# Two product lengths of an input unit, alternated or in two blocks

## The chip, the cores and the metric

The kernel runs on one core of a Trainium2 chip. A core has a matrix engine (TensorE, PE in the profile, with its weight loads as PEld), a vector engine (VectorE, DVE), a scalar engine (ScalarE, ACT), a general engine (GpSimd, POOL) and a queue for transfers (SyncE, SP). They run side by side and wait for one another by semaphores. The metric is device time in microseconds; the median of three runs of the kernel before is 1085.15 us (1085.05 to 1085.44).

## The reference

Three layers act on a sequence of 256 tokens with 1024 features, all in float32. The first has sliding-window attention and a feed-forward part, the second a gated mixing of chunks (gating stage below) and a feed-forward part, the third a mixer of a state-space scan and attention, and an MLP. The parts that the change touches:

```python
def conv_gated_ffn(h, w_in, conv_w, conv_b, w_out):
    S = h.shape[1]
    g, u = jnp.split(h @ w_in, 2, axis=-1)
    gp = jnp.pad(g, ((0, 0), (CONV_WIDTH - 1, 0), (0, 0)))
    g = conv_b + sum(conv_w[k] * gp[:, k:k + S] for k in range(CONV_WIDTH))
    return (jax.nn.gelu(g) * u) @ w_out

def chunked_sgu(h, w_in, ln_g, ln_b, w_s, b_s, w_out):
    z = jax.nn.gelu(h @ w_in)
    u, v = jnp.split(z, 2, axis=-1)
    ...
    return (u * sv.reshape(B, S, SGU_HALF)) @ w_out
...
    f = jnp.square(jax.nn.relu(h @ w_up[i])) @ w_down[i]
```

The inner size of a feed-forward part is 2816 (22 tiles of 128, each with a gate and an up half), that of the gating stage's u half 3072 (24 tiles), that of the MLP 4096 (32 tiles).

## The kernel before

All weights stream through a ring of six buffers in units of 128 partitions by 1024 values. SyncE loads a unit into `raw`; ScalarE rounds it to the short format of the matrix engine (`w_hi`, line 151); VectorE subtracts to get the rest (`w_lo`, line 156). The activations are kept in the same two parts, `a_hi` and `a_lo`, side by side in one tensor `both`. A product of two float32 numbers is then the sum of three: hi x hi, hi x lo and lo x hi.

`features_apart` computes one unit of an input projection: 128 output features for 256 tokens, a sum over KT = 8 slices of 128 input features. Its stationary operand is a slice of the weights. Since `w_hi` meets both parts of the activations, one product of 512 columns takes both at once (the two halves of a PSUM bank); `w_lo` meets `a_hi` alone, in a product of 256 columns that adds to the first half. The two halves are added later by ScalarE and VectorE. So a unit is sixteen products, eight long (line 198) and eight short (line 200), here called pairs. `pre` is given by no caller.

Who calls it: the feed-forward loop of `ffn_pe` (two units for tile t, gate and up, then `accumulate` for the down projection of tile t - 2, twelve products of 512 columns at line 251); the gating stage, 24 units, twenty of them in a row (`u_unit`); `mlp_pe` (one unit for tile t, then twelve products for an earlier tile). That makes 42 + 42 + 24 + 30 = 138 units. The last tiles of a feed-forward part and of the MLP are held: their input units stand together, and the down projections follow in one block.

The order on each engine is written out by hand. A unit waits for `lo_done` (its `w_lo` is ready) before its first product, and its last product raises `unit_used`, which lets ScalarE overwrite the ring buffer and read the results. The other products of the kernel are `three` (lines 173 to 175), which uses 256 columns for features and 512 or 256 for tokens.

Of the kernel before, what the change touches and what calls it, by code (L numbers as in the profile page):

```python
# [13 lines left out]
P = 128  # L14
SEQ = 256
TT = SEQ // P
D = 1024
KT = D // P
# [68 lines left out]
def build(nc, w, x_in, cols_in, misc_in, tables_in, rows_in, ws_in, wdt_in, out):  # L87
    def sb(name, shape, dt=F32):
        return nc.alloc_sbuf_tensor(name, shape, dt)
# [9 lines left out]
    w_hi = sb("w_hi", [P, RING, UNIT], F32R)  # L99
    w_lo = sb("w_lo", [P, RING, UNIT], F32R)  # L100
# [3 lines left out]
    both = sb("both", [P, 2, 2 * KT, SEQ], F32R)  # L104
    a_hi, a_lo = both[:, 0], both[:, 1]
# [10 lines left out]
    ps = nc.alloc_psum_tensor("ps", [P, 8, 512], F32)  # L116
# [73 lines left out]
    def features_apart(pe, n, bank, i=0, pre=None):  # L190

        s = n % RING
        pe.wait_ge(lo_done, n + 1 + RING * i)
        for k in range(KT):
            if pre is not None:
                pe.wait_ge(pre.lo, pre.base + k + 1)
            c = slice(k * P, (k + 1) * P)
            pe.matmul(ps[:, bank, :].rearrange("p (h t) -> p h t", h=2), w_hi[:, s, c], both[:, :, k, :],  # L198
                      start=k == 0, stop=False)
            mm = pe.matmul(ps[:, bank, 0:SEQ], w_lo[:, s, c], a_hi[:, k, :], start=False, stop=k == KT - 1)  # L200
        mm.then_inc(unit_used, 1)

    def features_tile(pe, n, bank, tt, pre, ks=range(KT)):
# [176 lines left out]
    def tile(tt):  # L380
        return slice(tt * P, (tt + 1) * P)
# [196 lines left out]
    def ffn_in_pe(pe, f, n0, t, i=0):  # L578
        if t >= 3:
            pe.wait_ge(f.summed, t - 1 + 2 * i)  # L580
        g_bank, u_bank = f_banks(t, i)
        features_apart(pe, f_g(n0, t), g_bank, i)
        features_apart(pe, f_g(n0, t) + 1, u_bank, i)
# [5 lines left out]
    def ffn_pe(pe, f, n0, u, following, turn_early=True):  # L589
        entry_pe(pe, u, n0, f_banks(0, 0))  # L590
        features_apart(pe, f_g(n0, 1), f_banks(1, 0)[0])
        row_pe(pe, u, 2)
        features_apart(pe, f_g(n0, 1) + 1, f_banks(1, 0)[1])
        ffn_in_pe(pe, f, n0, 2)
        pe.wait_ge(next_sems.row_out, f_row[f])
        pe.wait_ge(f.lo, 1)
        accumulate(pe, f_out(n0, 0), f_slot(0), True, False)
        ffn_in_pe(pe, f, n0, 3)
        pe.wait_ge(f.lo, 2)
        accumulate(pe, f_out(n0, 1), f_slot(1), False, False)  # L600
        with pe.Fori(0, (FT - 6) // 2) as i:
            for t in (4, 5):
                ffn_in_pe(pe, f, n0, t, i)
                pe.wait_ge(f.lo, t - 1 + 2 * i)
                accumulate(pe, f_out(n0, t - 2), f_slot(t), False, False, i)
        ffn_in_pe(pe, f, n0, FT - 2)
        ffn_in_pe(pe, f, n0, FT - 1)
        held = [(f_out(n0, t), f_slot(t)) for t in range(FT - HELD, FT)]
        held_pe(pe, following, held, lambda slot: pe.wait_ge(f.lo, FT - HELD + [s for _, s in held].index(slot) + 1), turn_early)
# [1882 lines left out]
```

## Time and profile before

| | |
|---|---|
| median of 3 runs | 1085.15 us |
| the profiled execution | 1085.08 us, span 1083.1 us |
| TensorE busy | 1064.0 us, 98% |
| weight loads | 902.2 us, 83% |
| VectorE | 820.6 us, 76% |
| ScalarE | 673.4 us, 62% |
| GpSimd | 39.8 us, 4% |
| DMA, mean over the span | 171 GB/s |

Busy time is the union of an engine's instructions. A matmul's recorded time overlaps the next one's, so the number of products times a mean duration is more than the time that they take. The distance between two starts, which a timeline gives, is the pace.

### The profile page before, as it was taken

The page shows a single profiled execution, that of the slowest core. Times are in us where ns is not written, and L with a number is a line of the kernel's source. Part 1 is how long each engine was busy: PE and PEld are TensorE (multiplying, and loading weights), DVE is VectorE, ACT ScalarE, POOL GpSimd, SP SyncE. Part 2 cuts the span into 40 slices and gives each one's busy share as a digit, 9 for nine tenths or more (in the row PEclk, how much of TensorE's full clock was granted, in tenths as well). Part 3 has the DMA queues.
Part 4 walks back from the last instruction along what each step waited for, and adds up shares of the span by engine and source line. Part 5 has one row for each costly group of instructions (what it writes and reads, how often), then busy time and mean ns, then how long its engine had stood idle before and what let it go on. Part 6 is the DMA issues. An engine that isn't in the chain of part 4 may idle for free. (4 is left out here: it accounts for less than half of the span.)

```text
span 1083.1 us, 18647 instructions
## 1 busy us (share of the span) xinstructions
PE 1064.0 (98%) x6022; PEld 902.2 (83%) x6022; DVE 820.6 (76%) x1460; ACT 673.4 (62%) x1270; POOL 39.8 (4%) x71
## 2 busy tenths in 40 slices
PE   7999999999999999999999999999999999999997
PEld 7978888888788888888888888899668888888886
DVE  6777998888754678877998888798779749666664
ACT  6567564555765867666554555777877747445553
POOL 0010000000010002220000000000000000000000
PEclk9999999999999999999999999999999999999999
DMA  8363666556366565443665565264212545655541
GB/s 333 130 230 127 204 201 206 175 191 196 118 233 202 168 213 169 162 169 112 204 203 204 175 193 195 81 220 167 78 40 82 184 145 173 201 188 186 185 151 40
DMA packets 51380, 185.04 MB, mean 171 GB/s; under 512 B 5728, under 2 KB 6240, under 8 KB 51328
## 3 DMA queue, kind: packets, MB, share of 16 engines
q1 hardware_dynamic: 49248, 178.28, 49.1%
q0 software_dynamic: 1504, 5.44, 1.4%
q8 instruction: 31, 0.51, 0.2%
q10 hardware_dynamic: 576, 0.64, 0.2%
q14 instruction: 21, 0.17, 0.1%
HBM read 183.29 MB, written 1.05 MB: 170 GB/s over the span
## 5 line engine op out<-in xcount | busy, mean ns | idle before, releaser
L156 DVE TENSOR_TENSOR w_lo<-raw,w_hi 128x1024 fp32r<-128x1024 f32 x336 | 411.7, 1233 | 74.2 <-ACT w_hi L151 70.8
L151 ACT ACTIVATE w_hi<-raw 128x1024 fp32r<-128x1024 f32 x336 | 350.8, 1053 | 70.6 <-PE ps L251 44.5
L198 PE MATMUL ps<-both,w_hi 128*128 128x512 f32 x1104 | 392.3, 398 | 0.9 <-DVE arena L656 0.9
L200 PE MATMUL ps<-both,w_lo 128*128 128x256 f32 x1104 | 309.7, 281 | 0.0
L251 PE MATMUL ps<-w_hi,both 128*128 128x512 f32 x992 | 292.9, 395 | 1.1 <-DVE both L2209 0.5
L198 PEld LDWEIGHTS ps<-both,w_hi 128*128 128x128 f32 x1104 | 207.3, 188 | 51.7 <-DVE arena L656 1.8
L251 PEld LDWEIGHTS ps<-w_hi,both 128*128 128x128 f32 x992 | 178.8, 188 | 39.1 <-issue 1.2
L200 PEld LDWEIGHTS ps<-both,w_lo 128*128 128x128 f32 x1104 | 208.4, 189 | 2.5
L251 PE MATMUL ps<-w_lo,both 128*128 128x512 f32 x496 | 158.2, 392 | 0.0
L251 PEld LDWEIGHTS ps<-w_lo,both 128*128 128x128 f32 x496 | 93.1, 188 | 21.2
L621 ACT ACTIVATE arena<-arena 128x256 f32<-128x256 f32 x44 | 18.4, 419 | 98.9 <-DVE arena L652 98.9
L173 PE MATMUL ps<-both,w_hi 128*128 128x256 f32 x256 | 74.2, 290 | 1.0 <-DVE arena L424 0.7
L174 PE MATMUL ps<-both,w_hi 128*128 128x256 f32 x256 | 72.4, 283 | 0.0
L175 PE MATMUL ps<-both,w_lo 128*128 128x256 f32 x256 | 72.4, 283 | 0.0
L173 PE MATMUL ps<-w_hi,both 128*128 128x512 f32 (+1 forms) x160 | 61.2, 382 | 0.6 <-DVE both L460 0.6
L175 PE MATMUL ps<-w_hi,both 128*128 128x512 f32 (+1 forms) x160 | 59.1, 369 | 0.0
L174 PE MATMUL ps<-w_lo,both 128*128 128x512 f32 (+1 forms) x160 | 59.0, 369 | 0.0
L173 PEld LDWEIGHTS ps<-both,w_hi 128*128 128x128 f32 x256 | 48.9, 191 | 3.8 <-issue 2.4
L652 DVE SCALAR_TENSOR_TENSOR arena<-pad,cols,arena 128x256 f32<-128x256 f32 x88 | 42.7, 485 | 10.2 <-DVE arena L648 0.3
L174 PEld LDWEIGHTS ps<-both,w_hi 128*128 128x128 f32 x256 | 49.0, 191 | 0.2
L175 PEld LDWEIGHTS ps<-both,w_lo 128*128 128x128 f32 x256 | 48.9, 191 | 0.0
L2190 ACT ACTIVATE arena<-ps 128x256 f32<-128x256 f32 x32 | 12.2, 382 | 49.8 <-PE ps L200 49.8
(212 smaller groups left out, 1206.8 us busy)
## 6 DMA issues: line engine op xcount, KB each, us to landing
raw<-in_w SPq DMA_DIRECT2D x336, 512.0 KB, 3.4
row<-in_rows POOLq DMA_DIRECT2D x7, 512.0 KB, 4.4
x<-in_x SPq DMA_DIRECT2D x2, 512.0 KB, 4.4
out<-x SPq DMA_DIRECT2D x4, 256.0 KB, 2.0
misc<-in_misc POOLq DMA_DIRECT2D x1, 512.0 KB, 6.1
arena<-in_ws POOLq DMA_DIRECT2D x1, 512.0 KB, 9.1
tab<-in_tables POOLq DMA_DIRECT2D x1, 320.0 KB, 4.8
tab<-in_tables POOLq DMA_DIRECT2D x1, 256.0 KB, 5.3
```

The lines of the kernel that those rows point to most:

```text
L151: act.activation(w_hi[:, s, :], raw[:, s, :], ACT.Copy).then_inc(hi_done, 1)
L156: dve.tensor_tensor(w_lo[:, s, :], raw[:, s, :], w_hi[:, s, :].bitcast(F32), ALU.subtract).then_inc(lo_done, 1)
L173: pe.matmul(o, l_hi, r_hi, start=first, stop=False)
L174: pe.matmul(o, l_hi, r_lo, start=False, stop=False)
L175: return pe.matmul(o, l_lo, r_hi, start=False, stop=last)
L198: pe.matmul(ps[:, bank, :].rearrange("p (h t) -> p h t", h=2), w_hi[:, s, c], both[:, :, k, :], start=k == 0, stop=False)
L200: mm = pe.matmul(ps[:, bank, 0:SEQ], w_lo[:, s, c], a_hi[:, k, :], start=False, stop=k == KT - 1)
L251: mm = pe.matmul(ps[:, 2 * tt + c, :], a[:, slot, t], b[:, s, c * 512:(c + 1) * 512], start=f, stop=z)
L621: act.activation(F_GL[:, b, :], F_CV[:, b, :], ACT.Gelu_apprx_tanh).then_inc(f.gelu, 1)
L652: dve.scalar_tensor_tensor(F_CV[:, b, :], pad[:, b, k:k + SEQ], col(k), F_CV[:, b, :], ALU.mult, ALU.add).then_inc(f.conv, 1)
L2190: act.activation(M_PT[:, t % 3, :], ps[:, m_bank(t, i), SEQ:2 * SEQ], ACT.Copy).then_inc(m_sem.part, 1)
```

## The change

The one loop over k becomes two: the eight products with `w_hi` first, then the eight with `w_lo`. The slice `c` is written as `tile(k)`, which is the same slice.

```diff
--- before.py
+++ after.py
@@ -194,10 +194,10 @@
         for k in range(KT):
             if pre is not None:
                 pe.wait_ge(pre.lo, pre.base + k + 1)
-            c = slice(k * P, (k + 1) * P)
-            pe.matmul(ps[:, bank, :].rearrange("p (h t) -> p h t", h=2), w_hi[:, s, c], both[:, :, k, :],
+            pe.matmul(ps[:, bank, :].rearrange("p (h t) -> p h t", h=2), w_hi[:, s, tile(k)], both[:, :, k, :],
                       start=k == 0, stop=False)
-            mm = pe.matmul(ps[:, bank, 0:SEQ], w_lo[:, s, c], a_hi[:, k, :], start=False, stop=k == KT - 1)
+        for k in range(KT):
+            mm = pe.matmul(ps[:, bank, 0:SEQ], w_lo[:, s, tile(k)], a_hi[:, k, :], start=False, stop=k == KT - 1)
         mm.then_inc(unit_used, 1)
 
     def features_tile(pe, n, bank, tt, pre, ks=range(KT)):
```

The order on TensorE in the MLP loop, before: the end of one down projection and the start of the next unit (`mlp_lo` and `mlp_summed` are raised by VectorE).

```order
L251 MATMUL ps<-w_hi,both 128x512 x2
L193 REGISTER_ALU [waits mlp_summed]
L198 MATMUL ps<-both,w_hi 128x512 [waits lo_done]
L200 MATMUL ps<-both,w_lo 128x256
L198 MATMUL ps<-both,w_hi 128x512
L200 MATMUL ps<-both,w_lo 128x256
L198 MATMUL ps<-both,w_hi 128x512
L200 MATMUL ps<-both,w_lo 128x256
```

The pairs go on until there are eight. The same place after:

```order
L251 MATMUL ps<-w_hi,both 128x512 x2
L193 REGISTER_ALU [waits mlp_summed]
L197 MATMUL ps<-both,w_hi 128x512 [waits lo_done]
L197 MATMUL ps<-both,w_hi 128x512 x7
L200 MATMUL ps<-both,w_lo 128x256 x8
L2169 REGISTER_ALU
L245 REGISTER_ALU [waits mlp_lo]
L251 MATMUL ps<-w_hi,both 128x512 [waits lo_done]
```

The long products of the unit now follow the long ones of line 251 without a short one between them, and the short ones stand in one block ahead of the next down projection. The wait for `lo_done` is where it was. 

Where units follow each other directly, TensorE at tile 2 of the first feed-forward, from the gate unit to the up unit, before:

```order
L200 MATMUL ps<-both,w_lo 128x256
L198 MATMUL ps<-both,w_hi 128x512
L200 MATMUL ps<-both,w_lo 128x256
L198 MATMUL ps<-both,w_hi 128x512 [waits lo_done]
L200 MATMUL ps<-both,w_lo 128x256
L198 MATMUL ps<-both,w_hi 128x512
```

and after:

```order
L200 MATMUL ps<-both,w_lo 128x256 x8
L197 MATMUL ps<-both,w_hi 128x512 [waits lo_done]
L197 MATMUL ps<-both,w_hi 128x512 x7
L200 MATMUL ps<-both,w_lo 128x256 x8
L251 MATMUL ps<-w_hi,both 128x512 [waits lo_done,ffn0_lo,next_row_out]
```

Here a block of short products is followed by the long block of the next unit. The gating stage has twenty units in this way. VectorE, ScalarE, GpSimd and the transfer queue have the same instructions in the same order as before.

## Rows read from the trace of the kernel before

**Rows 1.** The page: busy us (share) x instructions; the granted clock in 40 slices.
```profile
PE 1064.0 (98%) x6022; PEld 902.2 (83%) x6022; DVE 820.6 (76%) x1460; ACT 673.4 (62%) x1270; POOL 39.8 (4%) x71
...
PEclk9999999999999999999999999999999999999999
```

**Rows 2.** The page, costliest groups: busy us, mean ns; idle before, releaser.
```profile
L198 PE MATMUL ps<-both,w_hi 128*128 128x512 f32 x1104 | 392.3, 398 | 0.9 <-DVE arena L656 0.9
L200 PE MATMUL ps<-both,w_lo 128*128 128x256 f32 x1104 | 309.7, 281 | 0.0
```

**Rows 3.** Waits of TensorE: us in total, times, longest us.
```profile
PE ps L281 <- DMA tab<-in_tables: 4.7, 1, 4.7
...
PE ps L198 <- DVE arena L656: 0.9, 2, 0.5
```

**Rows 4.** Busy time by windows: a feed-forward turn, an MLP turn.
```profile
core 0: us, PE busy (x) PEld busy (x) DVE busy (x) ACT busy (x) POOL busy (x), PEclk, DMA share, GB/s
132.90:141.28 8.38, 8.38 (x45) 7.15 (x44) 7.35 (x13) 4.22 (x7) 0.00 (x0) 1.00 0.63 207
943.42:949.01 5.59, 5.59 (x30) 4.70 (x28) 3.63 (x6) 2.81 (x4) 0.00 (x0) 1.00 0.56 188
```

**Rows 5.** Timeline of TensorE (start us, us), end of the MLP.
```profile
1072.43 0.62 PE L251 MATMUL ps<-w_hi,both 128*128 128x512 f32 x2
...
1077.19 0.39 PE L251 MATMUL ps<-w_hi,both 128*128 128x512 f32 x1
```

**Rows 6.** The same in the second mixer, two lengths in blocks.
```profile
720.70 0.40 PE L173 MATMUL ps<-w_hi,both 128*128 128x512 f32 x1
...
722.54 0.39 PE L175 MATMUL ps<-w_hi,both 128*128 128x512 f32 x1
...
723.45 0.28 PE L173 MATMUL ps<-both,w_hi 128*128 128x256 f32 x1
...
724.40 0.28 PE L175 MATMUL ps<-both,w_lo 128*128 128x256 f32 x1
...
726.32 0.38 PE L1491 MATMUL ps<-tab,arena 128*128 128x128 f32 x2
```

**Rows 7.** The same in the gating stage.
```profile
360.75 0.40 PE L198 MATMUL ps<-both,w_hi 128*128 128x512 f32 x1
...
364.28 0.40 PE L198 MATMUL ps<-both,w_hi 128*128 128x512 f32 x1
```

**Rows 8.** The same in the first units of a feed-forward.
```profile
104.95 0.39 PE L198 MATMUL ps<-both,w_hi 128*128 128x512 f32 x1
...
112.58 0.63 PE L251 MATMUL ps<-w_hi,both 128*128 128x512 f32 x2
```

**Rows 9.** The same in one turn of the MLP loop.
```profile
943.42 0.39 PE L198 MATMUL ps<-both,w_hi 128*128 128x512 f32 x1
943.64 0.28 PE L200 MATMUL ps<-both,w_lo 128*128 128x256 f32 x1
...
944.11 0.40 PE L198 MATMUL ps<-both,w_hi 128*128 128x512 f32 x1
944.35 0.28 PE L200 MATMUL ps<-both,w_lo 128*128 128x256 f32 x1
944.47 0.40 PE L198 MATMUL ps<-both,w_hi 128*128 128x512 f32 x1
...
946.23 0.64 PE L251 MATMUL ps<-w_hi,both 128*128 128x512 f32 x2
...
948.09 0.63 PE L251 MATMUL ps<-w_lo,both 128*128 128x512 f32 x2
...
949.01 0.39 PE L198 MATMUL ps<-both,w_hi 128*128 128x512 f32 x1
```

**Rows 10.** The same, first products of two feed-forward turns.
```profile
132.90 0.39 PE L198 MATMUL ps<-both,w_hi 128*128 128x512 f32 x1
...
141.28 0.39 PE L198 MATMUL ps<-both,w_hi 128*128 128x512 f32 x1
```

## The prediction

> **What bounds the kernel now.** I read the page's busy shares first: TensorE is busy 1064.0 of 1083.1 us, 98%, VectorE 76%, ScalarE 62% [rows 1]. The clock digits are all nines and each stage I asked for has a granted clock of 1.00, the 2.4 GHz level [rows 1, 4]. So a gain has to come from TensorE's own pace, and it arrives at the end unless another engine takes its place. Next the waits of TensorE: the longest is 4.7 us for the first table, and at the two lines that the change touches there are 0.9 us in all [rows 3]. The windows then show the inner loops: in one turn of a feed-forward pair of units and in one of an MLP unit TensorE is busy without a hole (8.38 of 8.38 us, 5.59 of 5.59), while VectorE has 7.35 and 3.63 of work and the DMA share is 0.63 and 0.56 [rows 4]. TensorE is the bound there, with about 1 us to spare on VectorE in the tighter of the two.
>
> A busy sum can't price this change: matmuls overlap, the mean of one is 398 ns for 512 columns and 281 ns for 256 [rows 2], yet a pair takes much less than 679 ns. What counts is the distance from start to start, so I took starts from timelines.
>
> **The paces that the trace shows.** (a) A settled stream of 512-column products: 21 of them between 1072.43 and 1077.19, 4.76 us, 0.2267 each [rows 5]. (b) A stream of 256-column products: 24 from 723.45 to 726.32, 2.87 us, 0.120 each; the first eight behind a long block take 0.95 [rows 6]. (c) 512-column products directly behind 256-column ones: the first eight take 1.84 (720.70 to 722.54), the next four 0.91, so 0.03 us is lost at the start of such a block and nothing later [rows 6]. Eight settled ones take 8 x 0.2267 = 1.81. (d) The alternation of today: ten pairs from 360.75 to 364.28 take 3.53, 0.353 a pair [rows 7]; (a) and (b) add to 0.2267 + 0.120 = 0.347. So changing length at each instruction costs 0.006 us a pair. (e) Not everywhere: in the first units of a feed-forward, 22 pairs from 104.95 to 112.58 take 7.63, 0.347, the plain sum [rows 8]. This also tells me that the two-piece moving operand of the long product (the high and the low half of the activations) costs nothing of its own, since in (e) these same products run at the pace of (a) and (b). (f) The 512-column stream behind an alternating unit pays too: its first eight take 946.23 to 948.09, 1.86 [rows 9].
>
> **The change part by part.** It removes nothing and adds nothing: 1104 products of each length as before [rows 2]. The wait for the weights stays ahead of a unit's first product and the signal that the unit is used stays on its last; both loops run over the same weights. Each unit goes from eight pairs to one block of eight 512s and one of eight 256s. VectorE, ScalarE and the DMA queue keep their order; each of them only sees the end of the unit, which comes sooner. A unit now has one change to long and one to short in place of fifteen.
>
> MLP turn (one unit, then twelve long products of the down projection): now 943.42 to 949.01, 5.59 [rows 9]. After: the unit's long block follows a long stream, 1.81; its short block 0.95; the twelve behind it 1.84 + 0.91 = 2.75; sum 5.51. Saves 0.08. There are 28 such units: 2.2 us.
>
> Feed-forward turn (two units, then twelve): now 132.90 to 141.28, 8.38 [rows 10]. After: 1.81 + 0.95 for the first, 1.84 + 0.95 for the second (behind short ones), 2.75: 8.30. Saves 0.08; 17 turns in each of two layers: 34 x 0.08 = 2.7 us.
>
> Gating stage, twenty units in a row at pace (d): 8 x 0.353 = 2.82 each, after 1.84 + 0.95 = 2.79. Saves 0.03 x 20 = 0.7 us. (With a third digit, 2.824 against 2.79.)
>
> The last four units of a feed-forward, and the last two of the MLP, stand together in front of held products: 4 x 2.82 = 11.29 becomes 2.76 + 3 x 2.79 = 11.13, 0.16 twice, and 2 x 2.82 becomes 2.76 + 2.79, 0.1: 0.4 us in all.
>
> Units that already run at (e): four in each feed-forward and the last four of the gating stage, 12: 8 x 0.347 = 2.77 becomes 2.79. Costs 0.02 x 12 = 0.2 us.
>
> Sum: -2.2 - 2.7 - 0.7 - 0.4 + 0.2 = -5.8 us. The profiled execution took 1085.08 us, its span 1083.1 and 2.0 around it; the median of the runs is 1085.15, so nothing need be shifted. 1085.1 - 5.8 = 1079.3 us, 0.53% faster.
>
> Bounds of the one unknown. No row shows blocks of exactly eight and eight. If a change of length cost nothing, each unit would take 2.77 and the result would be lower by 0.03 us for each of 138 units with two changes, some 4 us less at most: 1075. If each long block of a unit paid what the eight of (f) pay, it would take 1.86 in place of 1.81 or 1.84, at most 0.05 x 138 = 6.9 us more, which eats the gain: 1086. I take (c), because it is the nearest row: the same two lengths, weights new for each product, in one accumulation after another.
>
> What hides the rest: the loops would run at 8.30 and 5.51, above VectorE's 7.35 and 3.63 [rows 4], so its work stays covered; at its own busy time it would bind only after another 0.9 us. Between stages TensorE waits for chains that start at its own last product, and those move with it.
>
> A rule to weigh: the Trainium skill, "TensorE: Matmul & The Clock Gate", section "Back-to-back issue gap", gives columns over 2.4 plus 2.5 ns at the full clock, by which a pair would take 325 ns in any order and the change would be worth nothing. Neither (a), 0.2267, nor the pair at 0.353 agrees: the trace has an excess per product, and one that depends on the order.
>
> **The rivals.** *No change.* The delay of a long product could belong to something other than the neighbour, so that each block of eight starts afresh as in (f): 1.86 + 0.95 = 2.81 against 2.82, and behind the short block the twelve still pay as today. Saves 0.01 x 138 = 1.4 at most; I put it at 1084.3. For it: the trace has two paces for the same alternation, (d) and (e), and I can't say what sets one or the other. Against it: rows 6 and 5 settle after a few products.
>
> *Slower.* One mechanism, at each unit: the weight load. A short product leaves little time to bring the next weights in. Now each short one is followed by a long one, under which a load fits easily; in a block of short ones each load stands under a short product, at 0.120 against the 0.117 at which the short ones go in the alternation (944.35 to 944.47, 0.12) [rows 9]. If the long ones keep what they have in a pair, 0.353 - 0.117 = 0.236 (944.11 to 944.35, 0.24), for a reason of their own, a unit takes 8 x 0.236 + 8 x 0.120 = 2.85 against 2.82: +0.024 x 126 units = +3.0, 1088.1 us. It decides where a long product inside a block stays above 0.233. For it: the short stream's 0.120 is measured. Against: (e), and the 0.2267 at a unit's edge, where a long product follows a long one (943.42 to 943.64).
>
> The Trainium skill speaks against the change here: "TensorE: Matmul & The Clock Gate", section "LDWEIGHTS (loading the stationary operand)", puts a load of 128 columns at 128 / 1.2 = 107 ns, as long as a 256-column product streams, so a block of short ones would have no slack at all; the same rule adds nothing beyond the 0.120 of (b), which is in the sum already.
>
> *Part of it is given back.* The feed-forward loops could fall on VectorE, whose 7.35 of 8.38 is a mean and has chains in it (convolution, gelu, product). Then 2.7 us stay away: 1082.0. Against: no wait of TensorE on VectorE shows inside a loop.
>
> **How the numbers follow.** Forecast 0.70, part given back 0.08, no change 0.13, slower 0.09. The smallest difference from no change that a measurement of this kernel can tell is about 0.2%, 2.2 us. Faster: 0.70 + 0.08, and nothing of the rest: 0.78; same 0.13; slower 0.09. The likeliest case alone spans 1077.3 to 1081.0. The range reaches up to the no-change case to leave out only the slower one and a tail: 1077.0 to 1084.6.
>
> **What would show it.** In the changed profile, a unit's eight long products behind a long stream should take 1.81 from its first start to the start of the short block, 1.84 behind short ones, the short block 0.95; the MLP turn 5.51, the feed-forward turn 8.30. Mean duration and count of the two groups say little. I am wrong if long products in the middle of a block stay at 0.235, if the turns are unchanged, or if TensorE shows waits on VectorE at the down projection's first product in the loops.

## The result

| | |
|---|---|
| changed kernel, median of 5 | 1079.27 us (1079.23 to 1079.37) |
| before, median of 5 beside it | 1085.15 us (1085.05 to 1085.46) |
| ratio | 0.9945 [0.9934, 0.9957] |
| profiled execution | span 1077.4 us (1083.1 before) |

The change makes the kernel 5.9 us, 0.55%, faster; the forecast was 5.8 us and 1079.3.

The page of the changed kernel, busy times and the groups of TensorE (as in [rows 1, 2]):

```profile
PE 1058.5 (98%) x6022; PEld 903.8 (84%) x6022; DVE 820.3 (76%) x1460; ACT 673.8 (63%) x1270; POOL 40.0 (4%) x71
...
L251 PE MATMUL ps<-w_hi,both 128*128 128x512 f32 x992 | 292.6, 395 | 1.1 <-DVE both L2209 0.5
L197 PE MATMUL ps<-both,w_hi 128*128 128x512 f32 x1104 | 275.4, 391 | 0.9 <-DVE arena L656 0.9
...
L200 PE MATMUL ps<-both,w_lo 128*128 128x256 f32 x1104 | 153.9, 282 | 0.0
```

TensorE is busy 5.5 us less and still 98% of the span. The groups show how little the busy column can tell of a pace: the short products go from 309.7 to 153.9 us and the long ones from 392.3 to 275.4, since products of one line that follow each other are now merged where they overlap. The means are 391 and 282 ns against 398 and 281 [rows 2]. The pace has to be read from starts. One turn of the MLP loop in the timeline of TensorE (start us, us; it answers to [rows 9]):

```profile
939.48 1.98 PE L197 MATMUL ps<-both,w_hi 128*128 128x512 f32 x8
941.29 1.11 PE L200 MATMUL ps<-both,w_lo 128*128 128x256 f32 x8
942.25 0.63 PE L251 MATMUL ps<-w_hi,both 128*128 128x512 f32 x2
...
944.09 0.62 PE L251 MATMUL ps<-w_lo,both 128*128 128x512 f32 x2
...
945.00 0.39 PE L197 MATMUL ps<-both,w_hi 128*128 128x512 f32 x1
```

Eight long products behind a long stream take 941.29 - 939.48 = 1.81, the eight short ones 942.25 - 941.29 = 0.96 (0.95 and a rounding), the first eight long ones behind them 1.84, and the turn 5.52 in place of 5.59. A feed-forward turn (answers to [rows 10]):

```profile
124.46 1.98 PE L197 MATMUL ps<-both,w_hi 128*128 128x512 f32 x8
126.28 1.12 PE L200 MATMUL ps<-both,w_lo 128*128 128x256 f32 x8
127.23 2.00 PE L197 MATMUL ps<-both,w_hi 128*128 128x512 f32 x8
129.07 1.12 PE L200 MATMUL ps<-both,w_lo 128*128 128x256 f32 x8
130.02 0.63 PE L251 MATMUL ps<-w_hi,both 128*128 128x512 f32 x2
...
132.77 0.39 PE L197 MATMUL ps<-both,w_hi 128*128 128x512 f32 x1
```

1.82, 0.95, 1.84, 0.95 and 2.75 add to 8.31; before it was 8.38. TensorE in this window, and VectorE beside it:

```profile
core 0: us, PE busy (x) PEld busy (x) DVE busy (x) ACT busy (x) POOL busy (x), PEclk, DMA share, GB/s
124.46:132.77 8.31, 8.31 (x46) 7.17 (x44) 7.90 (x14) 4.64 (x8) 0.00 (x0) 1.00 0.71 232
```

VectorE's 7.90 is 95% of this window, which lies near the stage's start, and TensorE still has no hole. The next turn (132.77 to 141.08) has 7.15.

Where the 5.7 us of the two spans lie, from starts in the two timelines: from the first product of a stage's first unit to the first product behind its last unit.

| stage, us | before | changed | moved | forecast |
|---|---|---|---|---|
| first feed-forward | 169.01 | 167.51 | -1.50 | -1.4 |
| gating, 24 units | 69.55 | 68.90 | -0.65 | -0.6 |
| second feed-forward | 168.86 | 167.53 | -1.33 | -1.4 |
| MLP | 163.06 | 160.78 | -2.28 | -2.3 |

### The profile page after: what moved, and what is told of

Read it like the earlier page. It is cut to its first block and busy times, and to the rows that moved or that the text cites. A ratio compares the mean times of both kernels' runs of the same rounds, so it can differ in the third digit from the quotient of the medians.

```text
span 1077.4 us, 18647 instructions
## 1 busy us (share of the span) xinstructions
PE 1058.5 (98%) x6022; PEld 903.8 (84%) x6022; DVE 820.3 (76%) x1460; ACT 673.8 (63%) x1270; POOL 40.0 (4%) x71
## 5 line engine op out<-in xcount | busy, mean ns | idle before, releaser
L197 PE MATMUL ps<-both,w_hi 128*128 128x512 f32 x1104 | 275.4, 391 | 0.9 <-DVE arena L656 0.9
L197 PEld LDWEIGHTS ps<-both,w_hi 128*128 128x128 f32 x1104 | 202.4, 188 | 40.7 <-DVE arena L656 1.7
L200 PEld LDWEIGHTS ps<-both,w_lo 128*128 128x128 f32 x1104 | 150.6, 190 | 10.8
L200 PE MATMUL ps<-both,w_lo 128*128 128x256 f32 x1104 | 153.9, 282 | 0.0
L175 PE MATMUL ps<-both,w_lo 128*128 128x256 f32 x256 | 72.4, 283 | 0.0
L173 PEld LDWEIGHTS ps<-both,w_hi 128*128 128x128 f32 x256 | 49.0, 191 | 3.6 <-issue 2.2
L174 PEld LDWEIGHTS ps<-both,w_hi 128*128 128x128 f32 x256 | 49.0, 192 | 0.2
L175 PEld LDWEIGHTS ps<-both,w_lo 128*128 128x128 f32 x256 | 49.0, 191 | 0.0
```

Source lines behind the costliest of these rows:

```text
L173: pe.matmul(o, l_hi, r_hi, start=first, stop=False)
L174: pe.matmul(o, l_hi, r_lo, start=False, stop=False)
L175: return pe.matmul(o, l_lo, r_hi, start=False, stop=last)
L200: mm = pe.matmul(ps[:, bank, 0:SEQ], w_lo[:, s, tile(k)], a_hi[:, k, :], start=False, stop=k == KT - 1)
```

## The experiments

Each stands against the kernel before, run beside it on the same chip. Below, a return is a change from short products to long ones, and the settled paces are (a) and (b) of the prediction. My theory is the forecast's: a long product behind short ones comes late, by an amount that dies away over some six of them, and each return pays this once. The rivals: something other than length costs (the change of the weight tensor, the columns of the bank), or only long blocks gain.

### One part alone: the MLP

```diff
 # mlp_pe
-            features_apart(pe, m_up(t), m_bank(t, i), i)
+            features_blocks(pe, m_up(t), m_bank(t, i), i)
 # features_blocks: the changed features_apart; all others keep the old one
```

> Only the MLP's 30 units go in two blocks; feed-forward and gating stay alternated. Theory (a change from short to long costs some 0.03 us at the start of the long block, wherever it is, and the stages are independent): the MLP turn goes from 5.59 to 5.51 us, the other turns stay at 8.38 and at 0.353 a pair, the time falls by 2.3 us to 1082.8. Rival (the gain comes from one stage's waits, or a gain in one stage is given back by the ring of weights in another): the turn is 5.51 but the total moves by less than 1.5 us.

Measured 1082.84 against 1085.0 (ratio 0.9979 [0.9970, 0.9988]): 2.2 us less, the MLP's share of the table. The first and the last row of a turn:

```profile
937.55 1.98 PE L210 MATMUL ps<-both,w_hi 128*128 128x512 f32 x8
...
943.06 0.39 PE L210 MATMUL ps<-both,w_hi 128*128 128x512 f32 x1
```

5.51. The other stages keep their lengths in its trace (169.00, 69.55 and 169.05), and what TensorE saves in the MLP arrives at the end, but for 0.1 us.

### Is it the weight tensor or the length? All products long

```diff
-            mm = pe.matmul(ps[:, bank, 0:SEQ], w_lo[:, s, tile(k)], a_hi[:, k, :], ...)
+            mm = pe.matmul(ps[:, bank, :].rearrange("p (h t) -> p h t", h=2), w_lo[:, s, tile(k)], both[:, :, k, :], ...)
```

once in the order of before and once in two blocks of eight.

> The order of before, but the product with the weights' low part takes both parts of the activations too, so that all sixteen products of a unit have 512 columns (one term more is summed than before). Theory (only a change of length costs): every product goes at 0.2267 inside a unit, a unit takes 3.63 whatever the order, and the time is that of the blocked order of the same products within 1 us; about 1085 + 138 x 0.81 = 1197 us. Rival (the price comes from changing between the two weight tensors at each product): the alternated kernel is slower than the blocked one by 5 to 7 us.

> All sixteen products of a unit have 512 columns as in the run beside it, eight with the high part of the weights first, then eight with the low part. Theory (only a change of length costs): 0.2267 a product, the same time as the alternated order within 1 us, about 1197 us. Rival (changing the weight tensor costs): faster than the alternated order by 5 to 7 us.

Measured 1191.68 (alternated) and 1191.53 (blocks), ratios to before 1.0979 [1.0962, 1.0996] and 1.0979 [1.0962, 1.0995]. The order makes no difference as soon as the lengths are equal. Alternated, gating stage, from one high product to the one eight pairs on:

```profile
420.19 0.39 PE L196 MATMUL ps<-both,w_hi 128*128 128x512 f32 x1
420.42 0.39 PE L199 MATMUL ps<-both,w_lo 128*128 128x512 f32 x1
...
423.82 0.39 PE L196 MATMUL ps<-both,w_hi 128*128 128x512 f32 x1
```

423.82 - 420.19 = 3.63 for sixteen products, 0.2267 each. In blocks, eight of them:

```profile
420.82 1.98 PE L196 MATMUL ps<-both,w_hi 128*128 128x512 f32 x8
422.63 1.75 PE L199 MATMUL ps<-both,w_lo 128*128 128x512 f32 x7
```

1.81. So changing between the two weight tensors at each product is free. The total is 5 us under my 1197: I had left out that the down projections no longer come behind short products and lose their own delay. The twelve take 949.01 - 946.23 = 2.78 in [rows 9] and 12 x 0.2267 = 2.72 here; at some 65 places that is 4 us. Most of the rest is rounding: a unit grew by 3.63 - 2.824 = 0.80 and not by 0.81, which is 1 us over 138 units.

### Is it the bank's columns?

```diff
-            mm = pe.matmul(ps[:, bank, 0:SEQ], w_lo[:, s, c], a_hi[:, k, :], ...)
+            mm = pe.matmul(ps[:, bank, SEQ:2 * SEQ], w_lo[:, s, c], a_hi[:, k, :], ...)
```

> The order of before; the short products add to the second half of the bank in place of the first (the halves are summed later, so the result is the same sum). Theory (length of the neighbours): nothing changes, 1085.1, 0.353 a pair. Rival (the price of the alternation comes from adding to columns of the bank that the long product has just written, or is still writing): the pace moves; with the second half the columns are the ones written last, so the pair gets longer, by over 0.005 us, and the time by over 5 us.

Measured 1085.26 against 1085.0, ratio 1.0001 [0.9992, 1.0010]. Ten pairs in the gating stage:

```profile
361.68 0.40 PE L196 MATMUL ps<-both,w_hi 128*128 128x512 f32 x1
...
365.21 0.40 PE L196 MATMUL ps<-both,w_hi 128*128 128x512 f32 x1
```

3.53, as in [rows 7]. Which half of the columns just written the short product adds to does not matter.

### The size of the blocks

```diff
+        for k0 in range(0, KT, G):
+            for k in range(k0, k0 + G):
                 pe.matmul(... w_hi ...)
+            for k in range(k0, k0 + G):
                 mm = pe.matmul(... w_lo ...)
```

with G = 4 and G = 2; G = 8 is the changed kernel.

> All units in the order 4 long, 4 short, 4 long, 4 short. Theory (the delay of long products dies away over about six of them, 6, 9, 2, 5, 4 ns): four long ones behind short ones take 0.930, four short ones 0.472, a unit behind short ones 2.80 against 2.79 with blocks of eight: 1.5 to 2 us slower than the blocks of eight, 1081.0. Rival 1 (a fixed price of 0.020 for each return to long): 2.81 a unit, 1082.0. Rival 2 (only blocks long enough to settle gain anything): 1085.

> All units in the order 2 long, 2 short, four times. Theory (dying delay): two long ones behind short ones 0.469, two short ones 0.232, a unit 2.80: 1081 to 1082. Rival 1 (a fixed price of 0.020 for each return to long): 4 x 0.020 = 0.08 a unit, more than the alternation's 0.05: 1087. Rival 2 (only long blocks gain): 1085.

Measured, against 1085.0: G = 4 1082.24 (0.9972 [0.9961, 0.9983]), G = 2 1078.44 (0.9938 [0.9924, 0.9952]). Both lie outside what I wrote for the theory, on opposite sides, and neither rival fits both: a fixed price of 0.020 gives 1082.0 for four, which is near, and 1087 for two, which is far off; "only long blocks gain" gives 1085 for either. The timelines tell where the theory went wrong. With G = 4, the second half of an MLP unit and the twelve behind it:

```profile
943.11 1.09 PE L196 MATMUL ps<-both,w_hi 128*128 128x512 f32 x4
944.04 0.63 PE L199 MATMUL ps<-both,w_lo 128*128 128x256 f32 x4
944.51 0.63 PE L250 MATMUL ps<-w_hi,both 128*128 128x512 f32 x2
...
946.37 0.62 PE L250 MATMUL ps<-w_lo,both 128*128 128x512 f32 x2
...
947.28 0.39 PE L196 MATMUL ps<-both,w_hi 128*128 128x512 f32 x1
```

Inside the unit the theory holds: four long ones behind short ones 0.93, four short ones 0.47. But the first eight long ones of the down projection take 1.86 and the twelve 2.77; with G = 8 they were 1.84 and 2.75. I had given the twelve the same delay whatever the block of short ones ahead of them. 0.02 at some 65 down projections is 1.3 us, and 1081.0 + 1.3 = 1082.3. With G = 2, one unit and the twelve behind it:

```profile
944.70 0.62 PE L196 MATMUL ps<-both,w_hi 128*128 128x512 f32 x2
...
945.39 0.63 PE L196 MATMUL ps<-both,w_hi 128*128 128x512 f32 x2
945.86 0.39 PE L199 MATMUL ps<-both,w_lo 128*128 128x256 f32 x2
946.08 0.63 PE L196 MATMUL ps<-both,w_hi 128*128 128x512 f32 x2
946.55 0.40 PE L199 MATMUL ps<-both,w_lo 128*128 128x256 f32 x2
946.78 0.63 PE L196 MATMUL ps<-both,w_hi 128*128 128x512 f32 x2
...
947.48 0.62 PE L250 MATMUL ps<-w_hi,both 128*128 128x512 f32 x2
...
949.30 0.62 PE L250 MATMUL ps<-w_lo,both 128*128 128x512 f32 x2
...
950.21 0.39 PE L196 MATMUL ps<-both,w_hi 128*128 128x512 f32 x1
```

A block of two and two goes at 0.69 to 0.70 (945.39, 946.08, 946.78); over the gating stage's twenty units the mean is 0.697, against 0.693 for the settled paces, so a return costs 0.003 to 0.004. Two long ones take 946.55 - 946.08 = 0.47 against 0.453, and the two short ones behind them gain most of it back, 0.23 against 0.24. With eight, the long block loses 0.03 and the short one gives back 0.01 at most, 0.020 a return. The eight long ones behind the unit take 949.30 - 947.48 = 1.82, not 1.84. All sizes side by side, means over a stage of each trace:

| us | unit behind a unit (gating) | twelve behind a unit (MLP) | MLP turn |
|---|---|---|---|
| alternated | 2.83 | 2.78 | 5.59 |
| blocks of two | 2.79 | 2.73 | 5.51 |
| blocks of four | 2.81 | 2.77 | 5.55 |
| blocks of eight | 2.79 | 2.75 | 5.51 |
| settled paces alone | 2.77 | 2.72 | 5.49 |

What decides how much of a delay is given back I can't say; the pattern in the starts is regular to 10 ns over whole stages, so it is no chance.

### The other pace of the alternation

```diff
+            if m == 0:
+                pe.matmul(ps[:, UB[0], 0:P], ident, ident, start=True, stop=True)
             features_apart(pe, N_SGU + m, UB[m % 3], i)
```

> The order of before, with one product of 128 columns (identity by identity, into the bank that the unit is about to start) ahead of the gating stage's first alternated unit. The trace of before has two paces for the same alternation, 0.353 behind a long stream and 0.347 behind products of 128 columns. Theory (the pace is set by what stood ahead of the first pair, and then keeps itself up): the twenty units in a row go at 0.347, 160 pairs x 0.0063 = 1.0 us less, 1084.2. Rival (the faster pace belongs to these places for another reason, such as the buffers or the other engines' work): 0.353 stays and the time is 1085.2 to 1085.3.

Measured 1084.47 against 1085.35, ratio 0.9992 [0.9983, 1.0001]. The total alone would not settle a difference of 0.08%; the timeline does:

```profile
351.92 0.38 PE L1115 MATMUL ps<-tab 128*128 128x128 f32 x2
352.06 0.48 PE L198 MATMUL ps<-both,w_hi 128*128 128x512 f32 x1
...
352.49 0.39 PE L198 MATMUL ps<-both,w_hi 128*128 128x512 f32 x1
...
407.62 0.61 PE L1090 MATMUL ps<-arena 128*128 128x128 f32 x4
```

From the second pair to the end of the twentieth unit are 159 pairs: 407.62 - 352.49 = 55.13, 0.3467 each, against 0.353 in the same place before [rows 7]. One source line's product of 128 columns (the profile shows it as two instructions, x2 at 351.92) ahead of 320 products changed the pace of all of them; the stage took 68.59 us in place of 69.55. So the alternation has two rhythms that keep themselves up; behind a long stream it falls into the slower one, in which the pairs come 0.35, 0.35 and 0.36 apart, over and over. The faster one is the pace of (e), whose units stand behind products of 128 columns too.

### Pairs of units

```diff
+    def features_pair(pe, n, banks, i=0):
+        for j in range(2):          # gate, then up
+            s = (n + j) % RING
+            pe.wait_ge(lo_done, n + j + 1 + RING * i)
+            ... eight with w_hi into banks[j]
+        for j in range(2):
+            ... eight with w_lo into banks[j], then_inc(unit_used, 1)
```

> The changed kernel with the gate and the up unit of a feed-forward tile taken together from tile 2 on: eight long of the gate, eight long of the up, eight short of the gate, eight short of the up. One return to long products less in each of 40 tiles. Theory (0.020 us for each such return, the dying delay less what the first short product gives back): 8.28 a turn in place of 8.30, 0.8 us less than the changed kernel, 1078.5. Rival (the low part of the up unit's weights and the gate's result come too late in this order): TensorE waits in the loop, and the time is 1080 or more.

Measured 1082.28 against 1085.35, ratio 0.9971 [0.9959, 0.9982]: 3 us worse than the changed kernel, as the rival said, but not where it said. The turn is as short as the theory had it but for 0.01, 132.65 - 124.36 = 8.29:

```profile
124.36 3.79 PE L209 MATMUL ps<-both,w_hi 128*128 128x512 f32 x16
127.99 2.08 PE L214 MATMUL ps<-both,w_lo 128*128 128x256 f32 x16
129.90 0.63 PE L265 MATMUL ps<-w_hi,both 128*128 128x512 f32 x2
...
132.65 0.39 PE L209 MATMUL ps<-both,w_hi 128*128 128x512 f32 x1
```

The loss is at the held down projections: each feed-forward stage is 0.35 shorter (167.16 for 167.51), and what follows it is 1.8 longer. The wait of TensorE and, in the first feed-forward, what ended it:

```profile
PE ps L265 <- DVE both L675: 3.0, 2, 1.5
```

```profile
273.37 0.42 DVE L675 TENSOR_TENSOR both<-arena,both 128x256 fp32r<-128x256 f32 x1
...
273.84 0.74 PE L265 MATMUL ps<-w_hi,both 128*128 128x512 f32 x2 [1.52 <-DVE both L675]
```

The last activations of tile 21 come from VectorE at 273.37 + 0.42 = 273.79, and TensorE starts at 273.84, after 1.52 us of idle. The changed kernel has this point too:

```profile
271.99 0.42 DVE L662 TENSOR_TENSOR both<-arena,both 128x256 fp32r<-128x256 f32 x1
272.17 1.09 PE L251 MATMUL ps<-w_hi,both 128*128 128x512 f32 x4
...
274.25 0.40 PE L251 MATMUL ps<-w_lo,both 128*128 128x512 f32 x1
```

There VectorE is done at 271.99 + 0.42 = 272.41, and the third product of the group at 272.17, the first that needs tile 21, starts two paces later, at 272.62. That looks like 0.2 us to spare, but it is not: in a down projection the activations are the stationary operand, so the weight load of that product waits for VectorE too. The load:

```profile
272.46 0.19 PEld L251 LDWEIGHTS ps<-w_hi,both 128*128 128x128 f32 x1
```

It starts 0.05 behind VectorE's end, as it does above after the 1.52 us of idle (273.84 - 273.79), and one pace behind the load before it (272.17) it was due at 272.40. In the kernel before, the same load starts at 273.91, 0.13 behind VectorE's end at 273.78. So the changed kernel is at the limit here already. Its product still starts on time, but the nine from 272.17 to 274.25 take 2.08 against 9 x 0.2267 = 2.04, a delay like the one behind short products, with long ones alone around it. In the second feed-forward the load starts 0.05 behind VectorE's end too, and the products behind it lose 0.03.

This wait is what is late next. So I gave the last two tiles their old order:

```diff
+        if t < FT - 2:
+            features_pair(pe, f_g(n0, t), (g_bank, u_bank), i)
+            return
```

> As the pairs of units, but the last two tiles of each feed-forward keep one unit after the other. Theory (the turns were shorter, 8.29, and the loss came from the held down projections, where TensorE waited 1.5 us in each feed-forward for the products of the last tiles, late because the gate's result was late): the wait is gone, the time is 0.6 us below the changed kernel, 1078.6. Rival (the waits come from the pairs of the loop): a wait of over 1 us stays at the held projections and the time is 1081 or more.

Measured 1080.63 against 1085.2, ratio 0.9958 [0.9945, 0.9972]. Neither side came true: the time is 1.4 us above the changed kernel's in the same runs. The wait is halved, not gone:

```profile
PE ps L265 <- DVE both L679: 1.5, 2, 0.8
```

So my reason was half of it. VectorE takes the steps of a tile in its written order, and it ends tile 19's steps later where tile 19's gate came in a pair; tiles 20 and 21 queue behind that. In the trace tile 19's last step ends at 260.22 (258.83 in the changed kernel), and tile 21's at 273.06, not at 272.41. TensorE, whose turns are shorter, reaches the place sooner as well.

### A version that takes both

The edit in words: `features_apart` takes blocks of two (G = 2), and a new `features_turns` keeps the order of before and is called by the gating stage, with the one product of 128 columns ahead of its first unit.

> Blocks of two in the feed-forwards and the MLP, and the gating stage alternated with one product of 128 columns ahead of its first unit. Theory (the two gains lie in different stages and add): the gating stage falls by 1.2 us as with the product alone, in place of the 0.75 that blocks of two gave there, so 0.45 less than blocks of two: 1078.0, and 1.2 less than the changed kernel in the same runs. Rival (blocks of two are no better than blocks of eight, their 1078.4 was the chip's): 1078.8 to 1079.3, within 0.6 of the changed kernel.

> The changed kernel as it is, beside the two others on the same chip, for a difference under 0.1% to be told. Theory: 1079.3, over both. Rival (it lies at or under them): 1078.5 or less.

On the same chip: the combined kernel 1078.68 (0.9943 [0.9929, 0.9956]), the changed kernel again 1079.21 (0.9945 [0.9932, 0.9959]), before 1085.2. The gating stage is 68.59 us in its trace, 68.78 with blocks of two alone, 68.90 in the changed kernel, so that gain is there, 0.2 us on blocks of two and not the 0.45 I wrote: the product alone had brought 0.96 and not 1.2. In whole it is 0.5 us under the changed kernel, less than the 1.2 of the theory and within the rival's 0.6, with intervals that overlap. Its stages are each shorter in the trace (167.26, 68.59, 167.27, 160.59), 1.0 us together. That it is faster than the changed kernel is likely, and not shown by the times; against blocks of two alone (0.9938, on another chip) the times show nothing. The changed kernel is not "over both" as I wrote: the pairs of units are slower, 1080.63.

## Why the prediction was right

*What bounds.* TensorE's own pace bound the kernel, and no stage gave a gain back: all four stages moved by the forecast within 0.1 us, and the MLP alone brought its own 2.2. The room on VectorE I put too high: the turn I read, with 7.35, is not the tightest, and the one before it (124.51 to 132.90) has 7.81 of 8.39.

*The terms.* Each block's time was read from another place with the same lengths [rows 5, 6] and came out the same: 1.81, 0.95 and 1.84. The MLP turn was put at 5.51 and is 5.52, the feed-forward turn at 8.30 and is 8.31.

*The unknown cost.* I took (c), the nearest row, between 1075 and 1086. It held for blocks of eight, and there is some luck in that: (c) stands behind a block of 48 short products, and nothing ahead of the result told that eight would be long enough to be like it. For other sizes the same reading failed: it gave 1081.0 for four (1082.24) and 1081 to 1082 for two (1078.44). With four the long stream behind the unit loses 0.02 more than behind eight, with two it loses less and most of a unit's delay is given back. The forecast was right in mechanism as far as unequal lengths side by side are the cause, which the kernels with equal lengths show; in what a return costs it was right for one size. What carries the delay was not tested. A weight load starts with the product before its own: in the kernel before, the load of the product at 141.62 starts at 141.51, together with a short product, and the load of the product at 141.51 starts at 141.29, together with a long one. So behind a short product it is 0.11 us ahead and behind a long one 0.22. At the held down projections a load that had waited for VectorE was followed by the same kind of delay, without a short product near. That speaks for the load and against length as such, but no run changed it alone.

*The rivals.* "Slower" rested on long products keeping 0.236 inside a block; they go at 0.2267 once settled. "No change" rested on each block starting afresh at 1.86; it starts at 1.81 behind long ones. "Part given back" did not happen in the loops, but I had its place wrong too: they have room, and it is the held down projections where VectorE is met first. There the changed kernel has no room left, and loses 0.03 to 0.04 us in each feed-forward. I had not looked there. The remark on the weight load can't be settled here: short products alone, once settled, keep 0.120. By that rule of the Trainium skill ("TensorE: Matmul & The Clock Gate", section "LDWEIGHTS (loading the stationary operand)") a load of 107 ns would fit under them. The trace records 0.19 us for each load, begun while the one before is still running, so its durations neither bear the figure out nor refute it.

## What to carry to other kernels

Where TensorE is 98% busy, price an edit by the distance between starts, not by busy time, and look for a place in the same trace where the new neighbours already stand together. Products of unequal length that alternate can cost some 2% more than their two settled paces add up to; try blocks, and try more than one size, since four was worse than two and eight here. Before you move a result later inside an engine's turn, look at the last turn of the loop: what follows it may need that result at once. And read the room at such a place from the weight load and not from the product, since the load waits too.

## What the runs showed of the hardware

- Settled paces at the granted clock of 1.00: 0.2267 us for 512 columns and 0.120 for 256, each with a weight load. With 512 columns the pace is the same whether the weight tensor changes at each product or not.
- The same alternation runs at 0.353 or 0.347 a pair for its whole length, by what stood ahead of it; a single product of 128 columns (two instructions in the profile) switched 160 pairs.
- A return from short to long products costs 0.020 us with blocks of eight, 0.017 with blocks of four and 0.003 to 0.004 with blocks of two, between units of the gating stage. Twelve long products behind a unit lose 0.06, 0.01, 0.05 and 0.03 us against the settled pace, behind single short products, blocks of two, of four and of eight. Why it depends on the size in this way stays open.
- In both feed-forwards of the changed kernel a weight load that had waited for VectorE, by 0.06 us at most, was followed by long products that came 0.03 to 0.04 us late in all.
